# Three rounded products for the dense scores, a short top-k for the first 128 rows, and a new order around the last gates

## The reference, cut to what matters

```
idx_score = einsum('bqhk,bqh->bqk', relu(rel), wi)          # -inf where key > query, +inf for key < 16
_, sel    = lax.top_k(idx_score, 128)                       # sparse branch: keys kept per query
lb = (einsum('bqhd,bkhd->bhqk', q_nope, k_nope)             # dense branch: 64 dimensions
      + einsum('bqhr,bkr->bhqk', q_pe, k_pe)) * scale_b     # and 32 rotary ones
ob = einsum('bhqk,bkhd->bqhd', softmax(lb), vb)
mixed = concatenate([oa * silu(ga), ob * silu(gb)])
out   = layer_norm(ALPHA * h + mixed @ w_out)
```

## Time and profile before

| | us |
|---|---|
| median of three executions | 359.12 |
| the profiled execution, whole | 358.49 |
| its span in the trace | 356.6 |
| PE busy | 333.8 |
| DVE busy | 230.1 |
| ACT busy | 171.4 |
| POOL busy | 160.9 |

### The profile page before, as it was taken

The page is one execution under the profiler, slowest core; times in us unless marked ns, Lnnn a source line. Parts: engine busy times, 40 slices in busy tenths (PEclk is TensorE's granted clock), DMA queues, the critical chain, the costliest instruction groups (busy, mean ns, idle before and its releaser), DMA issues.

```text
span 356.6 us, 6190 instructions
## 1 busy us (share of the span) xinstructions
PE 333.8 (94%) x2187; PEld 275.0 (77%) x2187; DVE 230.1 (65%) x618; ACT 171.4 (48%) x378; POOL 160.9 (45%) x140
## 2 busy tenths in 40 slices
PE   1899999999999899999999999999999999999990
PEld 1588887877888669786868887887888797997980
DVE  6762310299775989897976785448767755534666
ACT  4764633442553335547443644763776643612230
POOL 4432999686251613455303470743234231630563
PEclk9999999999999999999999999999999999999997
DMA  7373333249211222112100140531313230140033
GB/s 281 149 239 134 131 99 112 80 162 302 75 59 59 73 106 56 34 59 80 58 15 2 59 149 2 142 97 34 107 43 89 91 89 3 59 120 2 0 119 119
DMA packets 11566, 32.87 MB, mean 92 GB/s; under 512 B 2392, under 2 KB 2392, under 8 KB 11536
## 3 DMA queue, kind: packets, MB, share of 16 engines
q1 hardware_dynamic: 8944, 27.08, 22.7%
q10 hardware_dynamic: 2592, 5.40, 5.3%
HBM read 29.83 MB, written 4.81 MB: 97 GB/s over the span
## 4 chain that ended last, share of the span: by engine, by line
PE 85%; DVE 8%; issue 3%; ACT 2%; DMA 1%; DVEq 0%; SPq 0%; ACTq 0%
PE ps_j L1176 54%; PE ps_o L1420 6%; PE ps_s L1369 5%; PE ps_s L1377 3%; PE ps_j L1218 2%; PE ps_t L1390 2%; PE ps_s L1337 2%; PE ps_t L1395 1%; PE ps_s L1379 1%; DVE iw L1007 1%; PE ps_j L1229 1%; PE ps_j L1234 1%; DMA res<-in_x 1%; DVE tmp L983 1%; PE ps_t L1399 1%
## 5 line engine op out<-in xcount | busy, mean ns | idle before, releaser
L514 POOL TENSOR_TENSOR wl<-raw,wh 128x1024 fp32r<-128x1024 f32 (+2 forms) x33 | 77.2, 2348 | 93.4 <-ACT wh L521 93.3
L1176 PE MATMUL ps_j<-hh,wh 128*128 128x512 f32 (+2 forms) x224 | 80.1, 358 | 1.5 <-ACT v_b L724 1.4
L1176 PE MATMUL ps_j<-hl,wh 128*128 128x512 f32 (+2 forms) x224 | 77.9, 348 | 0.0
L1176 PE MATMUL ps_j<-hh,wl 128*128 128x512 f32 (+2 forms) x224 | 77.7, 347 | 0.0
L644 POOL TENSOR_SCALAR pr<-pr,rden 128x528 f32<-128x528 f32 (+1 forms) x64 | 34.2, 552 | 54.2 <-DVE rden L1065 54.2
L1176 PEld LDWEIGHTS ps_j<-hh,wh 128*128 128x128 f32 (+1 forms) x224 | 41.9, 187 | 11.9 <-issue 4.2
L1176 PEld LDWEIGHTS ps_j<-hh,wl 128*128 128x128 f32 (+1 forms) x224 | 41.8, 187 | 5.5
L1176 PEld LDWEIGHTS ps_j<-hl,wh 128*128 128x128 f32 (+1 forms) x224 | 41.8, 187 | 5.5 <-issue 0.2
L521 ACT ACTIVATE wh<-raw 128x1024 fp32r<-128x1024 f32 (+2 forms) x35 | 35.9, 1040 | 2.9 <-DMA raw<-in_weights 2.9
L1176 PE MATMUL ps_j<-wh,hh 128*128 128x256 f32 (+1 forms) x112 | 32.1, 286 | 1.1 <-DVE res L976 1.1
L1176 PE MATMUL ps_j<-wl,hh 128*128 128x256 f32 (+1 forms) x112 | 31.4, 280 | 0.0
(11 more groups left out here) (225 smaller groups left out, 758.4 us busy)
## 6 DMA issues: line engine op xcount, KB each, us to landing
raw<-in_weights SPq DMA_DIRECT2D x37, 512.0 KB, 3.4
bias_by_distance<-bias_vector ACTq DMA_DIRECT2D x1, 2624.0 KB, 13.7
bias<-bias_by_distance ACTq DMA_DIRECT2D x8, 264.0 KB, 2.7
res<-in_x SPq DMA_DIRECT2D x4, 512.0 KB, 4.7
out<-res SPq DMA_DIRECT2D x3, 512.0 KB, 2.6
pt<-in_ln_emb_g SPq DMA_DIRECT2D x1, 512.0 KB, 5.5
pt<-in_ln_emb_b SPq DMA_DIRECT2D x1, 512.0 KB, 6.8
q_b<-qpe ACTq DMA_DIRECT2D x8, 64.0 KB, 2.0
```

Source lines behind the costliest of these rows:

```text
L514: eng.tensor_tensor(ring_of(False, b), raw_of(b), ring_of(True, b).bitcast(F32), ALU.subtract).then_inc(done, 1)
L1176: last = pe.matmul(dst, a, b, start=n == 0 and part[0], stop=n == count - 1 and part[1])
```

## The change

1. `k_b` and `q_b` hold a rounded high and a low part for each of two heads. `S g` for the dense heads is three products per tile (high by high, low by high, high by low) in place of one float32 product.
2. ACT evicts the high parts of both heads of a `qn` or `kn` job, DVE makes both low parts from the bank and the high part, each after ACT's.
3. The rotary rows go through DRAM: qpe writes into `pr`, `ROPEH` (ACT) rounds, `ROPEL` (DVE) subtracts, `ROPED` (ACT) issues two DMAs of 256 KB to DRAM, and each QPE loads both parts from there. `KROWS` does the same for k's rotary rows on ACT and DVE, in place of POOL's copy.
4. For the first 128 rows `FLIP` writes the negated scores in reverse order into `drop`, two rounds take its 16 highest, and the mask is read back reversed; from round 2 on half 1 has two tiles.
5. The order around the last gates, worked out from the new `schedule()`: qpe 0, KROWS, ROPEH 0, ROPEL 0, gate 5, I 7, qpe 1, FLIP, ROPED 0, halves (0 0), (0 1), gate 6, half (1 0), uv 0 to uv 3, qn 0, ROPEH 1, ROPEL 1, weight blocks va 0 and va 1, halves (1 1), (2 0), gate 7, QPE 0, kn 0 0, kn 0 1, uv 4, ROPED 1, ZERO, halves (2 1), (3 0), (3 1), (4 0), va 0 0, S 0, X 0, half (4 1), R 0, halves (5 0), (5 1), va 0 1, S 1. Behind S 1 the order is the same as before.

```
@@ schedule
         if h == 6:
             job("qpe", 0)
+            order += [("KROWS",), ("ROPEH", 0), ("ROPEL", 0)]
...
     job("qpe", 1)
+    order += [("FLIP",), ("ROPED", 0)]
     pick(2)
-    job("gate", 6)
+    job("gate", 6, extra=0)
+    pick(1)
+    for t in range(4):
+        job("uv", 0, t, extra=0)
+    job("qn", 0, extra=0)
+    order += [("ROPEH", 1), ("ROPEL", 1)]
     need(BLOCKS[0], 2)
-    pick(5)
-    job("uv", 0, 0, extra=0)
-    job("uv", 0, 1, extra=0)
+    pick(2)
     job("gate", 7, extra=0)
-    job("uv", 0, 2, extra=0)
-    job("uv", 0, 3, extra=0)
-    order.append(("ZERO",))
-    job("qn", 0, extra=0)
+    order.append(("QPE", 0))
     job("kn", 0, 0, extra=0)
     job("kn", 0, 1, extra=0)
     job("uv", 0, 4, extra=0)
-    order.append(("QPE", 0))
-    pick(3)
+    order += [("ROPED", 1), ("ZERO",)]
+    pick(4)
...
         if g < HEADS and g % 2 == 0:
-            pick(1 if g == 0 else 2)
+            pick(2)
...
-         "qn": (1, 1), "kn": (1, 1), ...
+         "qn": (2, 2), "kn": (2, 2), ...
...
+DROP_ROUNDS = (P - PICKED) // 8
+TOPK_HALF = [lambda r: (3,), lambda r: (0, 1, 2) if r < DROP_ROUNDS else (1, 2)]
@@ POOL, KPE
-                    pool.tensor_copy(k1, k0).then_inc(kp, 1)
-                    pool.wait_ge(kp, 5)
@@ ACT
                     elif kind == "qn":
...
-                        act.activation(q_b[0:HD, 0, :], bank[0:HD, :], ACT.Copy, scale=-SCALE_B).then_inc(job_act, 1)
+                        for e in range(2):
+                            act.activation(q_b[0:HD, 0, e, :], bank[HD * e:HD * e + HD, :], ACT.Copy,
+                                           scale=-SCALE_B).then_inc(job_act, 1)
...
+                elif stage == "KROWS":
+                    act.wait_ge(kp, 4)
+                    for e in range(2):
+                        act.activation(k_b[HD:HD + ROPE, 0, e, :], k0, ACT.Copy).then_inc(kr_act, 1)
+                elif stage == "ROPEH":
+                    n = arg[0]
+                    act.wait_ge(rope_t, n + 1)
+                    act.activation(pr[:, 1, 512 * n:512 * n + 512].bitcast(F32R), pr[:, 0, 512 * n:512 * n + 512],
+                                   ACT.Copy).then_inc(rope_h, 1)
+                elif stage == "ROPED":
+                    n = arg[0]
+                    act.wait_ge(rope_h, n + 1)
+                    act.wait_ge(rope_l, n + 1)
+                    for v in range(2):
+                        act.dma_start(rope_dram[4 * n:4 * n + 4, :, v, :],
+                                      pr[:, 1 - v, 512 * n:512 * n + 512]).then_inc(rope_out[n], 16)
                 elif stage == "QPE":
                     n = arg[0]
-                    act.wait_ge(rope_t, n // 2 + 1)
+                    act.wait_ge(rope_out[n // 2], 32)
...
-                        act.dma_start(q_b[HD:HD + 32, e, :], qpe[r:r + 32, n // 2, :]).then_inc(qpe_in, 16)
+                        act.dma_start(q_b[HD:HD + ROPE, :, e, :].bitcast(F32), rope_dram[2 * n + e]).then_inc(qpe_in, 16)
...
                         if n == 0 and g < 2:
                             act.wait_ge(i_add, 4 * HEADS)
+                            act.wait_ge(rope_out[0], 32)
+                            act.wait_ge(rope_out[1], 32)
@@ DVE
                     elif kind == "qn":
...
-                        dve.tensor_scalar(q_b[0:HD, 1, :], bank[HD:P, :], -SCALE_B, None, ALU.mult).then_inc(job_dve, 1)
+                        for e in range(2):
+                            dve.wait_ge(job_act, BY_ACT[j] + e + 1)
+                            dve.scalar_tensor_tensor(out=q_b[0:HD, 1, e, :], in0=bank[HD * e:HD * e + HD, :], scalar=-SCALE_B,
+                                                     in1=q_b[0:HD, 0, e, :].bitcast(F32), op0=ALU.mult,
+                                                     op1=ALU.subtract).then_inc(job_dve, 1)
                     elif kind == "kn":
...
-                        dve.tensor_copy(k_b[0:HD, 1, 264 * m:264 * m + 264], bank[HD:P, 0:264]).then_inc(job_dve, 1)
+                        s = slice(264 * m, 264 * m + 264)
+                        for e in range(2):
+                            dve.wait_ge(job_act, BY_ACT[j] + e + 1)
+                            dve.tensor_tensor(k_b[0:HD, 1, e, s], bank[HD * e:HD * e + HD, 0:264],
+                                              k_b[0:HD, 0, e, s].bitcast(F32), ALU.subtract).then_inc(job_dve, 1)
...
+                elif stage == "KROWS":
+                    for e in range(2):
+                        dve.wait_ge(kr_act, e + 1)
+                        dve.tensor_tensor(k_b[HD:HD + ROPE, 1, e, :], k0, k_b[HD:HD + ROPE, 0, e, :].bitcast(F32),
+                                          ALU.subtract).then_inc(kr_dve, 1)
+                elif stage == "ROPEL":
+                    n = arg[0]
+                    dve.wait_ge(rope_h, n + 1)
+                    s = slice(512 * n, 512 * n + 512)
+                    dve.tensor_tensor(pr[:, 0, s].bitcast(F32R), pr[:, 0, s], pr[:, 1, s], ALU.subtract).then_inc(rope_l, 1)
+                elif stage == "FLIP":
+                    dve.wait_ge(i_add, 4 * HEADS)
+                    dve.tensor_scalar(drop_back, iw[:, IOFF[0]:IOFF[0] + P], -1.0, None, ALU.mult).then_inc(flipped, 1)
@@ PE, S of a dense head
-                                    pe.matmul(dst, q_b[:, e, i * P:(i + 1) * P], k_b[:, e, a:b], start=True,
-                                              stop=b <= c0)
+                                    for n, (x, y) in enumerate(((0, 0), (1, 0), (0, 1))):
+                                        last = pe.matmul(dst, q_b[:, x, e, i * P:(i + 1) * P], k_b[:, y, e, a:b],
+                                                         start=n == 0, stop=n == 2 and b <= c0)
```

More of the change, by code:

```diff
@@ L286, with topk_count @@
 LAST_IN_JOB = max(n for n, j in enumerate(JOBS) if j[0] not in ("out", "tq"))
-TOPK_HALF = [(3,), (0, 1, 2)]
+DROP_ROUNDS = (P - PICKED) // 8
+TOPK_HALF = [lambda r: (3,), lambda r: (0, 1, 2) if r < DROP_ROUNDS else (1, 2)]
+def topk_count(r, half):
+    return 2 * sum(len(TOPK_HALF[half](n)) for n in range(r))
 def build(nc, x, meta, ln_emb_g, ln_emb_b, rel_bias, ln_post_g, ln_post_b, weights, gains, onehot, cos_t,
           sin_t, out):
+    rope_dram = nc.dram_tensor("rope_rows", (HEADS, ROPE, 2, NQ), F32, kind="Internal").ap()
     vec_dram = nc.dram_tensor("bias_vector", (HEADS, VECW), F32, kind="Internal").ap()
@@ L326, in build @@
         wi = sb("wi", [P, QT, HEADS])
+        drop = sb("drop", [P, P])
         top8 = sb("top8", [P, QT, 8])
@@ L344, in build @@
         with ExitStack() as latent:
-            k_b = sb("k_b", [96, 2, T], into=latent)
-            q_b = sb("q_b", [96, 2, NQ], into=latent)
+            k_b = sb("k_b", [96, 2, 2, T], F32R, latent)
+            with ExitStack() as scratch:
+                kpe = sb("kpe", [96, 2, T], into=scratch)
+            q_b = sb("q_b", [96, 2, 2, NQ], F32R, latent)
             cqh = sb("cqh", [P, 2, NQ], F32R, latent)
@@ L449, in build @@
         kp = sem("kp")
+        kr_act = sem("kr_act")
+        kr_dve = sem("kr_dve")
+        rope_h = sem("rope_h")
+        rope_l = sem("rope_l")
+        rope_out = [sem("rope_out0"), sem("rope_out1")]
+        flipped = sem("flipped")
         squared = sem("squared")
@@ L704, in _ @@
                                            ACT.Copy).then_inc(job_act, 1)
-                        act.activation(k_b[HD:HD + ROPE, 1, 264 * m:264 * m + 264], bank[HD:HD + ROPE, 0:264],
+                        act.activation(k1[:, 264 * m:264 * m + 264], bank[HD:HD + ROPE, 0:264],
                                        ACT.Copy).then_inc(job_act, 1)
@@ L731, in _ @@
                             act.wait_ge(s_mm, 4 * n)
-                        act.activation(k_b[0:HD, 0, 264 * m:264 * m + 264], bank[0:HD, 0:264],
-                                       ACT.Copy).then_inc(job_act, 1)
+                        for e in range(2):
+                            act.activation(k_b[0:HD, 0, e, 264 * m:264 * m + 264], bank[HD * e:HD * e + HD, 0:264],
+                                           ACT.Copy).then_inc(job_act, 1)
                     elif kind == "va":
@@ L939, in _ @@
                         dve.wait_ge(normed, 3)
+                        dve.wait_ge(squared, 4)
+                        dve.wait_ge(ss_mm, 2)
                         if n:
@@ L948, in _ @@
                         dve.wait_ge(rope_m, n + 1)
-                        dve.tensor_tensor(qpe[:, n, :], tmp[:, 0, :], tmp[:, 1, :], ALU.add).then_inc(rope_t, 1)
+                        dve.tensor_tensor(pr[:, 0, 512 * n:512 * n + 512], tmp[:, 0, :], tmp[:, 1, :], ALU.add).then_inc(rope_t, 1)
                     elif kind == "qn":
@@ L978, in _ @@
                     dve.wait_ge(job_act, BY_ACT[NJ["kk", 0, 1] + 1])
-                    dve.stream_shuffle(k_b[HD:HD + ROPE, 0, :], k_b[HD:HD + ROPE, 1, :], SWAP).then_inc(kp, 1)
+                    dve.stream_shuffle(k0, k1, SWAP).then_inc(kp, 1)
```

(7 more changed lines are left out.)

33 lines of the change are left out of this document (17 added, 16 removed).

## The result

The changed kernel takes 363.12 us (median of its runs, 362.01 to 365.66); the kernel before took 359.21 us beside it (358.1 to 359.97). The ratio is 1.0116, interval 1.0078 to 1.0154: 3.9 us slower by the medians, 4.2 by the ratio. The forecast was 360.5 us and "no change" as the likeliest case. The time lies at the upper edge of the range, in the case "slower" that had 0.36. The profiled execution took 362.51 us with a span of 360.7, against 358.49 and 356.6 before.

What follows compares the result with a forecast made beforehand. PE was taken to bound the kernel (85% of the chain), with DVE late in heads 0 and 1. Gates 0, heads -2.0, head 1's wait +2.55 - 0.15, head 3 +0.9 + 0.1 gave +1.4, so 360.5 us; range 355.8 to 363.2.

Steps and rivals of the forecast that it cites:

- no change: Whole kernel: a difference under 0.5% (1.8 us, so 357.3 to 360.9 us); chance 0.44.
- slower: Whole kernel: a total above the 357.3 to 360.9 us that counted as no change; chance 0.36.
- Gates and head 0: 0 at the start of S 1: Last gates to head 1's scores: PE's 0.7 us gain is lost again to DVE's top-k; S 1 starts at 142.0 as before.
- The wait before kn 1 0: Head 1: late minima, two ACT evictions and DVE's second low part hold the bank; PE waits 2.55 us.
- From kn to S 2 it is about as long as before: Behind head 1: the 0.3 us wait on va goes, 0.15 net comes back, kn's last low part just late.
- The scores' -0.28 per head: Dense heads on PE: three rounded products save 0.28 us per head, 2.0 us over heads 1 to 7.
- no wait of PE for QPE's loads: Heads: QPE loads twice the bytes from DRAM, costing nothing up to 4 us.
- short halves that bring DVE time: Top-k on DVE: a short half costs 1.7 us from round 2 on, 5.4 us less in all.
- D: Dense scores: each of 15 products per head pays a weight load, +1.2 us per head, 372 us; chance 0.02.
- rivals A: DVE in time: the extra wait on low parts stays hidden, scores give -2.2 and gates -0.7, 356.2 us; chance 0.20.
- C: Head 1: minima come in time, only serial parts count, 1.3 of the 2.55 us wait, 359.2 us; chance 0.13.
- Rival B: Last gates: POOL's subtraction slows DVE's ROPEL 1 by 1.8 us, all reaching the end, 362.3 us; chance 0.17.

Runs made afterwards that it cites:

- e2: Changed kernel with top-k half (4 1) moved out of the stretch between S 0 and S 1, head 7 taking two halves; 362.74 us, ratio 1.0096.
- A: As a run: the changed kernel itself, against the kernel before; 363.12 us, ratio 1.0116.
- e11: Changed kernel with e9's order around the gates and e9's places for top-k halves, qn and kn in the heads unchanged; 358.44 us, ratio 0.9985.
- e1: Changed kernel with the old order around the last gates and half (4 1) back ahead of S 0; 363.98 us, ratio 1.0123.
- e9: Changed kernel reordered: long jobs cover evictions at the gates, kn and qn precede exponentials in heads 1, 3, 5, top-k halves moved later; 357.33 us, ratio 0.9959.
- e4: Changed kernel with dense scores as one float32 product of the high parts, low parts made but unused; 363.72 us, ratio 1.013.
- e5: Changed kernel with the qn jobs and their QPE ahead of the exponentials at heads 1, 3 and 5; 363.92 us, ratio 1.0094.
- e3: Changed kernel without DVE's low parts in qn and kn, all three products using high parts; 357.86 us, ratio 0.9961.
- e7: Changed kernel with QPE 0 behind uv 4 instead of ahead of kn 0 0; 362.55 us, ratio 1.0091.
- e6: Kernel before the change with only the short top-k added (FLIP, narrow tile), order and scores as before; 358.86 us, ratio 0.9993.
- e12: Changed kernel with e9's qn and kn order in the heads, gates and top-k halves unchanged; 360.69 us, ratio 1.0048.
- e8: e5 with another order at the gates meant to cover each drain, and seven halves of top-k ahead of S 0 instead of nine; 364.94 us, ratio 1.0173.

## Why the prediction was wrong

The mechanism, low parts made in series that PE waits for, was right. What failed is the sum's term for the gates, which I put at nothing, and the saving at the even heads. Of +3.55 us I had +1.4. The 2.15 between them, by the steps:

1. **"Gates and head 0: 0 at the start of S 1"** failed; it was +1.06. I let head 0's minima end DVE's queue at 139.0. They ran at 140.36, which is 139.75 less the 0.61. Two paths were late. On DVE's, the four low parts of kn ended at 133.93 instead of 132.7, less the 0.61 still 0.6 late, and top-k behind them at 140.20. On PE's, the scores of head 0 began 2.3 us later than forecast (138.59 less 0.61, for 135.7): uv 4 had waited for those low parts, and uv 4 and va took 5.36 us at the lower clock, where the same 27 products took 4.0 at full clock in e2 (133.57 to the 137.57 where its scores begin in the chain). In A PE then ran through to head 1 without a wait, so its own lateness set S 1; by e2 DVE's queue would have set it some 0.5 earlier, so taking PE's path away alone gives little. That both begin at the gates is what e11 points to: with other gates and with halves of top-k moved away from them the whole kernel is 4.7 us faster.
2. **The wait before kn 1 0**: forecast 2.55, measured 2.16 and a slower start behind it. From S 1 to kn 1 0 that is 0.26 less than forecast. The minima of head 1 came at 147.07, less the 0.61 146.5, for 146.0. The step stood, the 1.25 us for one more half of top-k included. I named half (4 1), and e2 shows that this one lay in DVE's idle time ahead of the reciprocals. But behind them A has two halves where the kernel before has one. With one there, e1 (old gates) and e11 (e9's gates) wait 0.77 and 0.75 before kn 1 0; with two, A and e2 wait 2.16 and 2.39. So some 1.4 us of the wait is the second half, and the rest the two serial operations each on ACT and DVE. (The 149.22 from which I counted is where the chain leaves PE; kn 1 0 itself began at 149.04.)
3. **"From kn to S 2 it is about as long as before"** failed by 0.24: the low parts of kn made PE wait 0.26 and then 0.36 instead of not at all. (The view gives no releaser for the 0.36; DVE's last low part ended at 155.69, the scores began at 155.79.)
4. **The scores' -0.28 per head** is right for head 1 and the other odd heads (2.41, e.g. S 5) and in e4's comparison. It isn't there at heads 2, 4 and 6 (2.64 to 2.66 for 2.67 to 2.68 before): in the chain their first six products take 0.97 instead of 0.72. PE's timeline has 0.97 for head 3 too (165.23), so the products aren't slower. In a running stream their first 0.25 us lie under the end of the product before; behind a wait (0.36, 0.36 and 0.10 here) they don't. Three times 0.25 us is most of the 1.11 that was lost behind S 2 against the forecast. Most of the rest is head 3, which cost 0.2 more than forecast: PE's wait on `q_b` was shorter (0.48 for 0.9, and ahead of kn 2 1, since kn 2 0 uses the other bank), the low parts of kn cost more (a wait of 0.36 and the start behind it, for 0.1).
5. **The clock** was no term. In the profiled execution it was mostly hidden. In others it may not have been: A's 365.66 us had a mean clock of 0.973, its 362.01 one of 0.989. But at 0.990 A took 362.86 and 364.13, so the mean clock alone doesn't say. e5's profile pays for it in the open.

Right were: the casts gone from PE's path; no wait of PE for QPE's loads in A (they appear once evictions no longer cover them, in e3 and e7); KROWS, ROPEL and FLIP hidden; short halves that bring DVE time, but no time at the end (e6); weight loads that stay hidden (D). The rivals A and C fell, since head 1's minima came late and PE's wait before kn 1 0 was 2.16 us. Rival B fell by luck, for ROPEL 1 ended at 127.48, and POOL's first subtraction began 0.06 us later:

```profile
126.80 0.68 DVE L1039 TENSOR_TENSOR pr<-pr 128x512 fp32r<-128x512 f32 x1
```

```profile
127.54 4.74 POOL L534 TENSOR_TENSOR wl<-raw,wh 128x1024 fp32r<-128x1024 f32 x2 [9.50 <-ACT wh L541]
```

Open stays what decides whether the clock falls: behind the same waits of 0.51 and 1.45 us at the gates it fell in the profiles of A, e5 and e12 and not in those of e2 and e4. Open too is why profiles differ by up to 1.6 us at the start of qpe 1 already, and how e11's gain divides between the order of the gates and the three halves of top-k that left them.

## What to carry to other kernels

When an eviction becomes two serial operations on two engines, don't only price the operations: look for the next job on the same PSUM bank, and put a long job between them; then look at what else stands in the evicting engine's queue there. Here the same instructions in another order took 357.3 instead of 363.1 us, with both done. Count a short wait of PE at more than its length: the start behind it cost 0.25 us each, and the clock may fall. And before a piece is moved out of a full engine's way, check that it isn't what fills the engine's wait for someone else: the half ahead of the reciprocals was free, the second one behind them cost 1.4 us.

## What the runs showed of the hardware

- A mean clock of 0.99 hides stretches at half clock. Behind 0.51 + 1.45 us of waiting PE ran about 3.5 us at 1.2 GHz in A's profile (256 columns every 0.21 us instead of 0.12), in e5 behind 1.2 us for about 7 us. In e2 and e4 the same 0.51 + 1.45 were followed by no such stretch.
- The first six score products count 0.97 us in the chain behind an idle PE and 0.72 in a running stream: in the stream 0.25 us of them overlap the product before.
- A DMA issue in ACT's queue took it 0.55 to 0.62 us for a load of `q_b` in A, and later activations stand behind it: 0.78 us of kn's first eviction in A, 2.36 us of the casts in e8, where one load's issue took 1.07.
- A DVE operation with two inputs in SBUF took 2.76 us beside POOL's subtraction (e9) and 0.69 without it (A).
- The 15 rounded products of 144 to 400 columns, each with a weight load of its own, took 0.27 us less at head 2 than the f32 products in the same place (2.64 in A for 2.91 in e4).
